# Attention stage of a hybrid decoder layer: the next head's projection placed before the transposes in TensorE's step

## What is computed

```python
z  = rms_norm(x, g_pre_mix) @ w_in           # q, k: 8 heads of 2 x 64 columns; v: 8 heads of 128
def block(args):                             # one block of 128 queries
    sc = jnp.einsum('bhcqd,bhckd->bhcqk', q_blk, kt).astype(jnp.float32)   # c = 0, 1
    sc = jnp.where(causal, sc, -jnp.inf)
    p = jax.nn.softmax(sc, axis=-1)
    p_diff = p[:, :, 0] - lam * p[:, :, 1]
    return jnp.einsum('bhqk,bhkv->bhqv', p_diff.astype(vt.dtype), vt)
o = rms_norm(o, subln_g) * (1.0 - lambda_init)
```

## Time and profile before

| | |
|---|---|
| median of three runs | 1931.7 us (1930.1 to 1932.99) |
| span of the profiled execution | 1929.6 us |
| TensorE matmuls, busy | 1886.7 us (98%) |
| TensorE weight loads, busy | 1558.5 us (81%) |
| VectorE, busy | 867.4 us (45%) |
| ScalarE, busy | 560.9 us (29%) |
| attention stage, first scores to last step | 134.9 to 502.5 us of the span |

### The profile page before, as it was taken

One profiled execution on the slowest core, in us unless ns is written; L12 is line 12 of the kernel. 1 busy time (PEld: TensorE's weight loads), 2 busy tenths in 40 slices (PEclk: granted clock), 3 DMA queues, 4 the chain that ended last, 5 costly groups with the idle time before them and its releaser, 6 DMA issues. The chain is left out here.

```text
span 1929.6 us, 24783 instructions
## 1 busy us (share of the span) xinstructions
PE 1886.7 (98%) x9048; PEld 1558.5 (81%) x9048; DVE 867.4 (45%) x1368; ACT 560.9 (29%) x1101; POOL 155.3 (8%) x378
## 2 busy tenths in 40 slices
PE   6999999999999999999999999999999999999998
PEld 5877777777888888888888788888888888888886
DVE  4228888888512263232221745332343334324426
ACT  4226666666520131111212233211111111211111
POOL 2111112111110000000000012100000000000002
PEclk9999999999999999999999999999999999999999
DMA  6221111111261111111111512211111111211114
GB/s 211 88 56 33 56 56 59 61 55 44 74 221 55 49 44 44 55 46 53 43 55 43 164 66 95 80 55 49 39 54 54 34 52 43 65 33 54 44 56 163
DMA packets 143257, 130.40 MB, mean 68 GB/s; under 512 B 4096, under 2 KB 127488, under 8 KB 142160
## 3 DMA queue, kind: packets, MB, share of 16 engines
q1 hardware_dynamic: 132032, 85.73, 14.7%
q0 software_dynamic: 10864, 42.69, 6.2%
q10 hardware_dynamic: 288, 1.05, 0.2%
HBM read 108.48 MB, written 20.97 MB: 67 GB/s over the span
## 5 line engine op out<-in xcount | busy, mean ns | idle before, releaser
L1458 PE MATMUL ps<-hn,ring 128*128 128x512 f32 x2112 | 481.0, 389 | 0.9 <-DVE ring L995 0.9
L1458 PEld LDWEIGHTS ps<-hn,ring 128*128 128x128 f32 x2112 | 396.2, 188 | 83.5 <-DVE ring L995 1.4
L1458 PE MATMUL ps<-xn,ring 128*128 128x512 f32 x1824 | 415.9, 389 | 0.0
L1458 PEld LDWEIGHTS ps<-xn,ring 128*128 128x128 f32 x1824 | 342.2, 188 | 71.2
L995 DVE TENSOR_TENSOR ring<-raw,ring 128x1024 fp32r<-128x1024 f32 x116 | 142.0, 1224 | 447.5 <-ACT ring L577 447.3
L1458 PE MATMUL ps<-w_d,hf 128*128 128x512 f32 x1008 | 230.3, 389 | 0.0
L1458 PEld LDWEIGHTS ps<-w_d,hf 128*128 128x128 f32 x1008 | 189.1, 188 | 39.6 <-DVE ff_sum L1426 0.4
L577 ACT ACTIVATE ring<-raw 128x1024 fp32r<-128x1024 f32 x116 | 122.1, 1053 | 326.7 <-PE ps L1458 316.5
L1524 PE MATMUL ps<-xn,ring 128*128 128x512 f32 x864 | 214.1, 398 | 1.4 <-DVE qt L1068 1.0
L1524 PEld LDWEIGHTS ps<-xn,ring 128*128 128x128 f32 x864 | 158.3, 189 | 33.0 <-issue 1.1
L1400 DVE TENSOR_TENSOR ff_sum<-ff_sum,ps 128x512 f32<-128x512 f32 x144 | 99.0, 688 | 85.0 <-PE ps L1458 84.7
(11 more groups left out here) (154 smaller groups left out, 1737.2 us busy)
## 6 DMA issues: line engine op xcount, KB each, us to landing
raw<-in_w_in_dram SPq DMA_DIRECT2D x58, 512.0 KB, 4.1
raw<-in_w_gate_up_dram SPq DMA_DIRECT2D x44, 512.0 KB, 3.9
raw<-in_w_down_dram SPq DMA_DIRECT2D x22, 512.0 KB, 3.4
y_scratch<-y_out POOLq DMA_DIRECT2D x8, 1024.0 KB, 4.2
ya<-y_scratch POOLq DMA_DIRECT2D x8, 1024.0 KB, 14.7
v_scratch<-v_out POOLq DMA_DIRECT2D x16, 256.0 KB, 2.3
v_raw<-v_scratch POOLq DMA_DIRECT2D x8, 512.0 KB, 4.7
raw<-in_w_attn_proj_dram SPq DMA_DIRECT2D x8, 512.0 KB, 4.0
```

Source lines behind the costliest of these rows:

```text
L1458: last = pe.matmul(ps[:, bank, :], lhs, rhs, start=i == 0, stop=i == len(pairs) - 1)
```

## The change

In TensorE's `step_of`, `proj_part` moves from behind `diff_transposed` to ahead of it. Nothing is added or removed, and the other engines' programs are the same. The steps with `lag` of 1 or more (the tail behind the last head) have no `proj_part` and keep their order. The lines of the kernel after have numbers lower by 18, because blank lines at its head are gone.

```diff
                     scores(par, i)
                 newer = (0, 0)
+                if not lag:
+                    proj_part(i // 4, i % 4)
                 if lag < 2 and not (first and i < 1):
                     before = (i - 1) % TT
                     diff_transposed(before)
...
                     pe.wait_ge(exp_done, 2 * HEADS * TT)
                     half_job(xn, 0)
-                if not lag:
-                    proj_part(i // 4, i % 4)
                 if lag < 3 and not (first and i < 2):
```

## The result

The kernel after takes 2048.31 us (median of 4 runs, 2046.4 to 2051.62) against 1932.35 us for the kernel before in the same comparison: a ratio of 1.0604, 95% interval 1.0589 to 1.0619. That is 116 us more. The forecast was 2017 us, from 1998 to 2034: the direction was right, the size was not.

What follows compares the result with a forecast made beforehand. TensorE was taken to bound the kernel, in a tight ring with VectorE and ScalarE. Steps summed to 10.8 us more a head, net 86 us on a 1929.6 span; with 2.1 for the median, 2017 us, range 1998 to 2034.

Steps and rivals of the forecast that it cites:

- the predicted lengths: Steps 0 to 7 of a head: 7.91, 5.48, 5.94, 6.17, 7.61, 7.31, 8.58 and 8.32 us.
- the bank wait: In even steps the projection waits for VectorE to take the projected half out, near 2 us in step 0.
- the ring: Scores, projection quarter, transposes, ScalarE's copies, two exponentials, next scores: a chain setting step length, 8.32 us in step 7.
- the sum: Step lengths added over a head: 57.3 us against 46.51, 10.8 us more; net 86 us over eight heads.
- the 26.7 us: Waits of TensorE's weight loads at the transposes over 8 heads, up to all of it given back.
- so I count nothing for the clock: TensorE's clock in the new stage: no loss, with 44.91 busy us spread over 57 and a longest pause of 1.95.
- 10.8 - 0.8 + 1.4: First head: 10.8 us more a head, less 0.8 for no step-0 loss, plus about 1.4 in step 1.
- The window from 10 to 20 us: Evidence on the clock: TensorE busy for 5.20 of 10 us there, granted clock 1.00.
- The rival that I built on the rule: Clock falls after pauses in step 0 and one more step, 2.62 us each, 42 us: 2059; chance 0.04.
- The second ring through VectorE: Rival: VectorE's low parts of `pt` late by 0.3 us in five steps a head, 12 us: 2029; chance 0.10.
- the bank wait costs nothing: Rival: projected half is out when the scores end, 3.8 us a head less, 30 in all: 1987; chance 0.06.
- the change is a gain: Rival: the ring doesn't bind, only covered waits count, 12 to 27 us less: about 1912; chance 0.03.

Runs made afterwards that it cites:

- early take-out: Kernel after, with the projected half taken out in odd steps ahead of ScalarE's copies and exponentials and VectorE's low parts and difference; 2005.15 us, ratio 1.0380.
- steps 3, 5, 7 alone: Kernel before, with the projection quarter ahead of the transposes in steps 3, 5 and 7 only; 1994.72 us, ratio 1.0325.
- every pause filled: Kernel after, with 33 extra never-read matmuls a head in all of TensorE's new pauses; 2032.49 us, ratio 1.0526.
- the second pause of step 0 filled: Kernel after, with 8 extra never-read matmuls in step 0 between the scores and the projection quarter; 2045.18 us, ratio 1.0581.
- step 0 alone: Kernel before, with the projection quarter ahead of the transposes in step 0 only; 1936.37 us, ratio 1.0024.
- step 0's two pauses filled: Kernel after, with 3 extra never-read matmuls ahead of step 0's scores and 8 between them and the projection quarter; 2048.49 us, ratio 1.0595.

## Why the prediction was wrong

**The bound and the waits were read rightly.** The waits of the transposes for `diff` are gone from heads 2 to 7, the scores wait for `e_t` in steps 3 to 7 and 0, the projection waits for its bank in even steps, 1.88 us in step 0, and in the last head in step 0 alone. In heads 2 to 7 of the kernel after, steps 1 to 5 and 7 are within 0.16 us of the predicted lengths, and so is step 6 where the clock does not fall. Taking the bank wait out, or the ring alone, changed the steps that the sum said (early take-out; steps 3, 5, 7 alone). One reading was too large without touching the sum: the 26.7 us of the earlier trace rows are waits of the weight loads, and in the same stretch of the kernel before the matmuls themselves idled for 10.8 us at the transposes.

```profile
PE ps L1466 <- DVE y_out L995: 6.4, 17, 0.7
PE ps L1466 <- DVE diff L1087: 4.4, 7, 0.6
```

**The step that failed is "so I count nothing for the clock".** Between the first scores and the last head's step 7, the kernel after needs 476.2 us and the one before 360.6. In heads 2 to 7 the loss is 88.9 us where 64.9 were predicted. Of the 24 us between them, 16.8 lie in six steps 0, which last 10.46 to 10.94 us instead of 7.91, and 4.3 in three steps 6, which last 10.1 instead of 8.7; the rest is 0.5 us a head of small terms. The first head, up to the second's start, lost 15.1 instead of 11.4 (10.8 - 0.8 + 1.4), with a step 4 of 10.50 us. With every pause filled the clock stayed at 1.00 and a head took 58.5 to 59.0 us instead of 57.3: so the sum itself was low by about 1 us a head, since some 0.35 us of the difference is overrun in steps 2 and 3. The clock carries the rest: against the kernel with every pause filled, the seven steps 0 are 17.3 us longer in all, the three steps 6 with a fall 4.4 and the first head's step 4 2.8, together 24 of the 30 missing us. At most half of the 67 us at the low clock is lost, 33 us, which agrees. In the prediction's terms, the clock was put at nothing and measured 24 us.

**Why it failed.** The window from 10 to 20 us is a single thin stretch near the start of the kernel, and the trace of before has no stretch with a pause in nearly every step. I took one row for a rule. I also judged each pause for itself, 1.95 us at most, where the experiments show that no single one decides. The rule of the Trainium skill that I weighed ("TensorE: Matmul & The Clock Gate", section "Why this matters for your kernels") was right in direction only: it advises against single gaps longer than any here, so by its words this kernel would have had no fall either, and the trace shows eleven in the stage with no wait over 1.9 us. Nor does a fall always lie in a pause: in the kernel after it fell inside one (376.40 to 376.80 us), with that pause filled it fell during the extra matmuls. The rival that I built on the rule named step 0 and one more step, priced 2.62 us each, and had 0.04 of the chance. A step 0 with a fall lasts 2.6 to 3.0 us more than predicted, and 2.3 to 2.7 more than with every pause filled; the "one more step" was there in three heads and the first, 11 falls instead of 16, so its 42 us came out at 24. That rival was the right mechanism at too high a price, and its 2059 us missed the measured 2048 by 11.

**The rivals.** The second ring through VectorE is there in small (14.3 us of waits of the y transpose for `pt`), but hidden behind the wait for `e_t` that follows it; it decides only once the exponentials are moved ahead, where it cost more in steps 5 to 7 than the ring it replaced, though the kernel as a whole took 38 us less than the kernel after. That the bank wait costs nothing, and that the change is a gain, were both wrong.

**What stays open.** Which run of pauses drops the clock is not settled. It fell 11 times in the stage of the kernel after; it fell with the second pause of step 0 filled, and stayed up in heads 2 to 7 of the early take-out, with waits for `e_t` of up to 1.6 us. Filling part of the pauses moved the falls to other steps. It stayed up with a pause of 1.16 us in every step 0 and hardly any other (step 0 alone). Why VectorE starts late in two heads was not tried either.

## What to carry to other kernels

In a ring of engines that are all near full, the place of a block of independent work is what hides someone else's latency: here the projection hid copies and exponentials between the transposes and the next scores, and in front of the transposes it hid only the waits that were there, 27 us of the weight loads and 11 us of the matmuls. Before moving such a block, write down for each of its two neighbours what is queued behind it on the other engines, and which bank it needs free; the one step in which the move pays can then be done alone, with its bank emptied in time (3 us gained, where the whole change lost 116). And a TensorE stage into which a change brings pauses has to be priced at both clocks, since the loss was then a quarter larger than the waits alone.

## What the runs showed of the hardware

- The granted clock fell from 1.00 to 0.50 in a stage whose longest single wait was 1.9 us and in which matmuls were under way for four fifths of the time: TensorE's waits of 95 us in all came with some 65 us at the low clock.
- A projection quarter lasted 3.0 us at the high level and 5.5 at the low one; where the clock came back before its end, it lasted 4.5 to 4.6 (step 0's two pauses filled, steps 4 and 6).
- More work made the kernel faster: 33 extra matmuls a head took 16 us off the time, because they kept the clock up; the same kind of matmuls in one or two of the pauses took off at most 3 us, and falls came in steps 4, 6 and 7 instead.
- The clock can fall while matmuls run: with the pause behind the scores filled, it fell within 0.6 us of the start of the extra matmuls (377.43; granted clock 0.80 in the window from 377.60 to 378.00, 0.50 behind it).
